# Transposed blocks with joined halves, a new opening and earlier combination in a two-stack transformer kernel

## The chip, the cores and the metric

The kernel runs on one core of a Trainium2 chip. The metric is the device time of one execution in microseconds (us); the figure compared is the median of several runs. A profile is one such execution recorded by the hardware profiler.

## The reference, cut to what matters

256 positions of width 1024 in fp32 go through two stacks of two layers each. In the first stack a layer is FFN, mixer, FFN:

```python
for l in range(DEPTH):                       # DEPTH = 2
    h = h + 0.5 * swiglu(rmsnorm(h, ffn1_norm[l]), ffn1_w_gate[l], ffn1_w_up[l], ffn1_w_down[l])
    u = rmsnorm(h, mix_norm[l])
    z = u @ w_in[l]                          # latent queries/keys, diff q/k/v, pool input, gates
    ...                                      # MLA, differential attention, pooling: three branches
    h = h + merged @ w_out[l]                # gated sum of the branches
    h = h + 0.5 * swiglu(rmsnorm(h, ffn2_norm[l]), ffn2_w_gate[l], ffn2_w_up[l], ffn2_w_down[l])
h = rmsnorm(h, final_norm)

def swiglu(x, w_gate, w_up, w_down):         # D_FF = 2816
    return (jax.nn.silu(x @ w_gate) * (x @ w_up)) @ w_down
```

In the second stack a layer has a mixer of three other branches (gated linear attention, a gated MLP over positions, plain causal attention), and an FFN of width 4096 with the square of relu, `square(relu(h @ w_ff1)) @ w_ff2`, with layer norms between. The weights are some 360 MB, each read once.

## The kernel before, in words

**Precision and products.** The inputs are fp32 and TensorE multiplies in its fp32r format. Every operand is therefore split into a high part (rounded to fp32r) and a low part (the rest), and each product is made of three: low weight x high x, high weight x high x, high weight x low x. For the weights ScalarE writes the high part `wh` (L1694) and VectorE the low part `wl` (L1898, `raw - wh`), in place of the raw data. A unit of weights is 128 x 2048 elements, 1 MB. There are six raw buffers (`NL`) and five high ones (`NH`), so a unit is fetched when the unit six before it is done, and its high part made when the one five before it is done.

**Two forms of product.** The token form (L1455, "tokens") keeps x as the stationary operand, 128 positions by 128 features, and moves 512 weight columns; its result has positions on the partitions. It is used where the result must be so, in the down projections, gates, branches and the first block of each FFN after a norm, and its result is turned by transposes where the next product needs features on the partitions. The transposed form (L1472, "features", planned by `turned_group`) keeps 128 x 128 of the weights stationary and moves x with all its 256 positions; its result has features on the partitions, two groups of 128 features by 256 positions in a PSUM bank. It makes the FFN's hidden values, and the queries and keys of the diff and linear attention (`dqT`, `dkT`, `gqT`, `gkT`) and the linear attention's gate (`ggT`). Its result needs no transposes: ScalarE applies SiLU from PSUM (L1698) or relu (L1702), VectorE multiplies (L1903, L1907) into `mn`, ScalarE and VectorE split that into `mh`, `ml` (L1707, L1913). The down projection reads these. `dqT` and the others are copied by ScalarE (L1749).

**The order.** A planner, `Plan`, writes one list of work items. Each engine's program walks that list and takes its own items, in this order and strictly one after another; waits are on semaphores. `tick()` is called after each block of TensorE work: it runs work put off (`flush`: an item put on `self.later` is run at the second flush after it), lets each of four lanes take a step (`pump`: attention heads, transposes of norms, tables), and puts the next conversions of weights in the list (`advance`: fetches, low parts of those whose high part is in the list, then high parts). In a group of token products `visits` alternates between the two tiles of 128 positions; at the start of a stage four visits of tile 0 come first, at the end of a stage tile 0 is finished first so that its norm runs while TensorE is on tile 1.

**Opening** (`start`). SyncE loads x tile 0, the identity, two units of the gate's weights (these are half units, 512 KB), x tile 1, and so on. GpSimd's queue loads the norm's gain, broadcast to all partitions (L1385). TensorE does twelve transposes of the identity (L1487, "wake"). ScalarE squares (L1720), GpSimd makes the inverse root (L1375, L1379), VectorE scales by it and the gain (L1929), TensorE turns (L1482), ScalarE and VectorE split (L1713, L1917).

**Diff attention** (`diff_pair`). Scores of two heads with two maps each (L1517, L1520) go to four side banks (4 to 7), VectorE takes the maxima (L2034 to L2042), ScalarE the exponentials (L1773, L1775), VectorE combines the two maps (L2047 to L2053, "combine"), TensorE turns the result (L1527) and weighs the values. `latent_kv` makes the keys and values of the MLA branch; its key copies are on VectorE (L2022) and ScalarE (L1768, L1769), and it ends with a tick.

## Time and profile before

| what | value |
| --- | --- |
| median of 3 runs | 2102.19 us (2100.53 to 2102.81) |
| profiled execution, its own time | 2103.13 us |
| span of its first to last instruction | 2101.3 us |
| TensorE busy | 2075.6 us, 99% of the span |
| VectorE, ScalarE, GpSimd busy | 1268.6, 1032.4, 90.5 us |
| mean granted TensorE clock | 0.998 of 2.4 GHz |
| DMA | 375.41 MB, 179 GB/s over the span |

A busy share counts the time in which at least one instruction of the engine was open. Matmuls overlap, so their mean duration is longer than the distance from one to the next. The chain of waits is followed back from the last instruction to what released it, and its pieces on one engine tell how long a number of instructions took in a row.

### The profile page before, as it was taken

How to read it: one execution, taken by the hardware profiler on the slowest of the kernel's cores; microseconds unless marked ns; L12 is line 12 of the kernel's file. 1: busy time of each engine (PE TensorE's matmuls, PEld its weight loads, DVE VectorE, ACT ScalarE, POOL GpSimd, SP SyncE). 2: the span in 40 equal slices, each digit the busy share in tenths (PEclk: the TensorE clock that was granted, in tenths of full speed). 3: DMA queues.
4: the chain of work that ended last, by engine and by line, in shares of the span. 5: the costliest groups of instructions: out<-in, count | busy, mean ns of one | idle time of the engine just before them, and what ended most of it. 6: DMA issues, size and time to landing. Idle time of an engine off the chain costs nothing.

```text
span 2101.3 us, 28959 instructions
## 1 busy us (share of the span) xinstructions
PE 2075.6 (99%) x12424; PEld 1836.6 (87%) x12424; DVE 1268.6 (60%) x1429; ACT 1032.4 (49%) x1301; POOL 90.5 (4%) x123
## 2 busy tenths in 40 slices
PE   7999999999999999999999999999999999999998
PEld 6999978889989898888899989888899888888897
DVE  5555587765455455686654465557755666567555
ACT  5444576454444444675443355643544466445442
POOL 1000100000000001000000000010100000100000
PEclk9999999999999999999999999999999999999999
DMA  8555544465555555444555464544665545455552
GB/s 290 187 182 174 174 146 155 140 211 188 191 193 204 185 185 189 138 150 152 187 202 192 161 226 140 178 142 167 231 193 187 200 143 180 156 172 194 190 190 80
DMA packets 178191, 375.41 MB, mean 179 GB/s; under 512 B 8480, under 2 KB 18848, under 8 KB 178064
## 3 DMA queue, kind: packets, MB, share of 16 engines
q1 hardware_dynamic: 174256, 360.67, 51.7%
q0 software_dynamic: 3808, 12.90, 1.9%
q8 instruction: 98, 1.61, 0.3%
q14 instruction: 29, 0.24, 0.0%
HBM read 372.49 MB, written 1.05 MB: 178 GB/s over the span
## 4 chain that ended last, share of the span: by engine, by line
PE 94%; DVE 2%; DMA 1%; ACT 1%; issue 1%; SPq 0%; POOLq 0%; POOL 0%; DVEq 0%; ACTq 0%
PE pb L1455 56%; PE pb L1472 32%; PE pb L1482 2%; DMA raw<-in_ffn_w_up_dram 1%; PE pb L1527 1%; ACT wh L1694 0%; PE pb L1598 0%; DVE wl L1898 0%; DVE lS L2034 0%; DVE st L2040 0%; DVE st L2039 0%; PE pb L1661 0%; PE pb L1597 0%; PE pb L1620 0%; PE pb L1585 0%
## 5 line engine op out<-in xcount | busy, mean ns | idle before, releaser
L1898 DVE TENSOR_TENSOR wl<-raw,wh 128x2048 fp32r<-128x2048 f32 (+3 forms) x348 | 780.5, 2249 | 286.0 <-ACT wh L1694 285.5
L1694 ACT ACTIVATE wh<-raw 128x2048 fp32r<-128x2048 f32 (+3 forms) x348 | 655.3, 1883 | 501.4 <-PE pb L1455 267.0
L1472 PE MATMUL pb<-xh,wl 128*128 128x256 f32 x1856 | 529.2, 285 | 0.0
L1472 PE MATMUL pb<-xh,wh 128*128 128x256 f32 x1856 | 525.7, 283 | 0.0
L1472 PE MATMUL pb<-xl,wh 128*128 128x256 f32 x1856 | 525.7, 283 | 0.0
L1455 PE MATMUL pb<-wl,xh 128*128 128x512 f32 x928 | 371.7, 400 | 2.5 <-DVE xl L1917 2.5
L1455 PE MATMUL pb<-wh,xl 128*128 128x512 f32 x928 | 362.4, 390 | 0.0
L1455 PE MATMUL pb<-wh,xh 128*128 128x512 f32 x928 | 361.6, 390 | 0.0
L1472 PEld LDWEIGHTS pb<-xh,wl 128*128 128x128 f32 x1856 | 356.8, 192 | 1.4 <-issue 0.7
L1472 PEld LDWEIGHTS pb<-xh,wh 128*128 128x128 f32 x1856 | 356.7, 192 | 0.8
L1472 PEld LDWEIGHTS pb<-xl,wh 128*128 128x128 f32 x1856 | 356.6, 192 | 0.0
L1455 PE MATMUL pb<-wl,mh 128*128 128x512 f32 x736 | 254.6, 392 | 0.2
L1455 PE MATMUL pb<-wh,ml 128*128 128x512 f32 x736 | 252.9, 389 | 0.0
L1455 PE MATMUL pb<-wh,mh 128*128 128x512 f32 x736 | 252.7, 389 | 0.0
L1455 PEld LDWEIGHTS pb<-wl,xh 128*128 128x128 f32 x928 | 175.2, 189 | 40.1 <-issue 3.3
L1455 PEld LDWEIGHTS pb<-wh,xl 128*128 128x128 f32 x928 | 175.0, 189 | 36.7
L1455 PEld LDWEIGHTS pb<-wh,xh 128*128 128x128 f32 x928 | 175.5, 189 | 32.8
L1455 PEld LDWEIGHTS pb<-wh,ml 128*128 128x128 f32 x736 | 138.1, 188 | 29.0
L1455 PEld LDWEIGHTS pb<-wh,mh 128*128 128x128 f32 x736 | 138.2, 188 | 28.4
L1455 PEld LDWEIGHTS pb<-wl,mh 128*128 128x128 f32 x736 | 137.1, 188 | 28.1 <-issue 1.0
L1922 DVE SCALAR_TENSOR_TENSOR h<-pb,h 128x512 f32<-128x512 f32 x72 | 48.1, 686 | 94.9 <-PE pb L1455 94.9
L1707 ACT ACTIVATE mh<-mn 128x512 fp32r<-128x512 f32 x60 | 38.0, 633 | 98.8 <-DVE mn L1903 77.9
(345 smaller groups left out, 1660.5 us busy)
## 6 DMA issues: line engine op xcount, KB each, us to landing
raw<-in_w_in_dram SPq DMA_DIRECT2D x100, 1024.0 KB, 5.2
raw<-in_w_ff_dram SPq DMA_DIRECT2D x64, 1024.0 KB, 5.3
raw<-in_ffn_w_up_dram SPq DMA_DIRECT2D x44, 1024.0 KB, 5.2
raw<-in_ffn_w_down_dram SPq DMA_DIRECT2D x44, 1024.0 KB, 4.9
raw<-in_ffn_w_gate_dram SPq DMA_DIRECT2D x42, 1024.0 KB, 5.2
raw<-in_w_branch_dram SPq DMA_DIRECT2D x24, 1024.0 KB, 5.0
raw<-in_w_out_dram SPq DMA_DIRECT2D x16, 1024.0 KB, 5.0
raw<-in_w_in_dram SPq DMA_DIRECT2D x4, 832.0 KB, 4.4
```

What stands on the lines that cost most here:

```text
L1455: ins = e.matmul(pb[b][:, 0:c1 - c0], x[:, s, cols], w[:, n, c0:c1], start=(it["first"] and n == 0 and q == 0), stop=(it["stop"] and n == ...
L1472: ins = e.matmul(o, w[:, n, c], x[:, it["kk"] + n, :], skip_group_check=True, start=(it["first"] and n == 0 and q == 0 and f % 2 == 0), st ...
L1482: ins = e.transpose(bank[:, c * P:c * P + P], m.tile(it["src"], c), ident[:, :])
L1527: ins = e.transpose(bank[:, c * P:c * P + P], Sb[:, c * P:c * P + P], ident[:, :])
L1694: e.activation(hi, raw, ACT.Copy).then_inc(m.high_done, 1)
L1707: e.activation(m.mh[:, s:s + 2, :].rearrange("p a s -> p (a s)"), m.pair_of(it["src"]), ACT.Copy).then_inc(m.split_high, 1)
L1898: e.tensor_tensor(lo, raw, hi.bitcast(F32), ALU.subtract).then_inc(m.low_done, 1)
L1922: e.scalar_tensor_tensor(o, bank[:, :], it["coef"], o, ALU.mult, ALU.add).then_inc(m.evac[use[0]], 1)
```

## The change

**Joined blocks.** `xh` and `xl` become two halves of one tile `x2` (128 x 8 x 2 x 256). A block ("wide", planned by `wide_group`) is one unit of 8 slots x 256 columns. For each half i of 128 columns there are eight products of the high weight with `xh` and `xl` side by side, 512 columns into a whole bank, and eight of the low weight with `xh`, 256 columns into the bank's first half. VectorE sums the bank's two halves into SBUF ("wadd"). SiLU then runs in place in SBUF ("wsilu"), put off by `later`; "wmul" multiplies; "wrelu" makes relu times itself in one instruction on VectorE; the split into `mh` and `ml` is put off too. `dqT`, `dkT`, `gqT`, `gkT`, `ggT` are written by wadd. The tanh of `ggT` goes through a scratch tile.

**Opening.** TensorE starts with products over 512 columns of a tile of ones ("wake", 4, then 3, then 4). The gain comes as one row of 4 KB through ScalarE's queue and is spread to all partitions by two fp32 products over 512 columns ("spread"); VectorE reads it from PSUM. The identity comes through ScalarE's queue. While `held` is set no conversions are planned by `advance`; `opening` places them and the turns of tile 1. Loads of gains and of the mixer's constants wait for its end and eight pumps (`once_open`).

**Others.** `combine` stands directly behind the softmax items. `latent_kv` ends with a flush and an advance, without a pump. In the last down group of an FFN the column halves alternate inside each group of four slots. A turn of `mn` comes one pump later. Bank choice in the FFNs alternates between main and side banks by quarters of 256 columns.

The diff, cut to its core:

```diff
@@ Memory
-        self.xh = A("xh", take(8192), [P, 8, S], F32R)
-        self.xl = A("xl", take(8192), [P, 8, S], F32R)
+        self.x2 = A("x2", take(16384), [P, 8, 2, S], F32R)
+        self.xh, self.xl = self.x2[:, :, 0, :], self.x2[:, :, 1, :]
...
@@ Plan
+        if self.held:
+            return
         while self.nlo < self.nhi:
             self.add("low", j=self.nlo)
...
-    def turned_group(self, X, keys, banks, epi, base=0, by_bank=True):
...
+    def wide_group(self, key, banks, epi):
+        j = self.take(key)
+        self.split(j)
+        need = self.need("X", range(8), [0, 1])
+        for i in range(2):
+            if i:
                 self.tick()
+            use = self.use(banks[i])
+            v = self.pe("wide", j=j, i=i, use=use, need=need)
+            epi(i, v["p"], use)
+        self.freed[j] = self.x_free = v["p"]
         self.tick()
...
+    def once_open(self, go):
+        def gen():
+            while self.held:
+                yield
+            for _ in range(8):
+                yield
+            go()
+        if self.held:
+            self.lanes[3].append(gen())
+        else:
+            go()
...
-                            for b in range(2) for i in range(size // 2)], end=True)
+                            for i in range(size // 2) for b in range(2)], end=True)
...
+                    for c in range(0, n, 256):
+                        side = (sum(chunks) + n0 - c0 - c) // 256 % 2 == 1
+                        q = c // 256
+                        self.wide_group((gate, (l,), 0, 8, c0 + c, 256), self.pair(0, side), self.gate_w(q))
+                        self.wide_group((up, (l,), 0, 8, c0 + c, 256), self.pair(1, side), self.up_w(q, slot + 2 * q))
...
+    def gate_w(self, q):
+        def epi(i, p, use):
+            self.add("wadd", dst=("sg", q), i=i, p=p, use=use, free=self.sg_free[q])
+            if i:
+                self.silu_n = self.next("silu")
+                self.later.append(lambda: self.add("wsilu", q=q, use=use))
         return epi
+    def up_w(self, q, slot):
+        def epi(i, p, use):
+            self.turn_due(q)
+            self.add("wadd", dst=("mn", q), i=i, p=p, use=use, free=self.mn_free[q])
+            if i:
+                n = self.next("product")
+                self.add("wmul", q=q, use=use, s=self.silu_n)
+                self.split_later(q, slot, n)
+        return epi
...
@@ start
+        self.held = True
+        self.advance()
+        self.pe("wake", n=4)
+        v = self.pe("spread")
+        self.pe("wake", n=3)
+        self.spread = v["p"]
...
+        ready = self.rms(0, g, halves=(0,))
         self.split_next()
+        self.turn("X", 0, 0, ("xn", 0, 0), 4, [ready[0]])
+        self.pe("wake", n=4)
+        self.rms_rest(0, g)
         self.split_next()
         for b in range(2):
             self.square(1, b)
+        self.lanes[0].append(self.opening(g, ready))
+    def opening(self, g, ready):
+        self.turn("X", 4, 0, ("xn", 0, 1), 4, [ready[1]])
+        self.split_next()
+        yield
+        ready = self.rms(1, g, halves=(0,))
+        self.split_next()
+        self.rms_rest(1, g)
+        yield
+        self.turn("X", 0, 1, ("xn", 1, 0), 4, [ready[0]])
+        yield
+        self.turn("X", 4, 1, ("xn", 1, 1), 4, [ready[1]])
+        self.held = False
+        for _ in range(4):
+            yield
         self.add("consts")
...
@@ diff_pair, latent_kv
-        self.quiet = True
-        yield
         for i in range(2):
             c.append(self.next("combined"))
             self.add("combine", i=i, l=l, n=n[2 * i + 1], c=c[i])
+        self.quiet = True
+        yield
...
-        self.tick()
+        self.flush()
+        self.advance()
...
@@ TensorE
+        elif k == "wide":
+            bank, c = pb[use[0]], slice(i * P, i * P + P)
...
+            for s in range(8):
+                e.matmul(bank[:, :], hi[:, s, c], m.x2[:, s, :, :].rearrange("p a s -> p (a s)"), start=(s == 0),
+                         stop=False, skip_group_check=True)
+            for s in range(8):
+                ins = e.matmul(bank[:, 0:S], lo[:, s, c], m.xh[:, s, :], start=False, stop=(s == 7),
+                               skip_group_check=True)
...
+        elif k == "spread":
+            pe.wait_ge(m.first_set, 1)
+            pe.wait_ge(m.row_landed, 16)
+            for q in range(2):
+                ins = e.matmul(pb[1 + 2 * q][:, :], m.first[:, :], m.gain_rows[:, 512 * q:512 * q + 512], start=True, stop=True)
...
@@ ScalarE
+            e.dma_start(m.ident[:, :], m.A["c_ident"]).then_inc(m.ident_landed, 16)
+            a.wait_ge(m.rows_set, 1)
+            e.dma_start(m.gain_rows[0:1, :], m.A["ffn1_norm"][0:1, :]).then_inc(m.row_landed, 16)
...
+            e.activation(m.sg[q][:, :], m.sg[q][:, :], ACT.Silu).then_inc(m.silu_done, 1)
...
@@ VectorE
+        elif k == "wadd":
+            v.pe(p)
+            v.ready(it["free"])
+            e.tensor_reduce(m.half(it["dst"], i), bank[:, :].rearrange("p (a s) -> p s a", a=2), AXX,
+                            ALU.add).then_inc(m.evac[use[0]], 1)
+        elif k == "wmul":
+            q = it["q"]
+            v.emptied(use)
+            v.wait_ge(m.silu_done, it["s"] + 1)
+            e.tensor_tensor(m.mn[q][:, :], m.mn[q][:, :], m.sg[q][:, :], ALU.mult).then_inc(m.product, 1)
+        elif k == "wrelu":
...
+            e.scalar_tensor_tensor(m.mn[q][:, :], m.sg[q][:, :], 0.0, m.sg[q][:, :], ALU.max,
+                                   ALU.mult).then_inc(m.product, 1)
```

## Rows read from the trace of the kernel before

**Rows 1.** The page: span, and busy time of TensorE and its loads.
```profile
span 2101.3 us, 28959 instructions
...
PE 2075.6 (99%) x12424; PEld 1836.6 (87%) x12424; DVE 1268.6 (60%) x1429; ACT 1032.4 (49%) x1301; POOL 90.5 (4%) x123
```

**Rows 2.** The page's groups: line, operation, count, busy us, mean ns, idle before.
```profile
L1472 PE MATMUL pb<-xh,wl 128*128 128x256 f32 x1856 | 529.2, 285 | 0.0
...
L1455 PE MATMUL pb<-wl,xh 128*128 128x512 f32 x928 | 371.7, 400 | 2.5 <-DVE xl L1917 2.5
```

**Rows 3.** Chain of waits, 0 to 320 us: start us, us, what, how many.
```profile
49.50 40.32 PE pb L1472 x336
89.82 32.67 PE pb L1455 x144
122.49 57.59 PE pb L1472 x480
```

**Rows 4.** Waits of TensorE: us in total, times, longest.
```profile
PE pb L1517 <- ACT kT L1769: 4.0, 2, 2.0
PE pb L1455 <- DVE xl L1917: 2.5, 2, 1.4
PE pb L1482 <- DVE xn L1929: 2.4, 1, 2.4
PE pb L1527 <- DVE lS L2053: 2.4, 5, 0.6
PE pb L1482 <- DVE mn L1903: 1.9, 1, 1.9
```

**Rows 5.** VectorE's groups by shape, columns as in the page's groups.
```profile
L1898 DVE TENSOR_TENSOR wl<-raw,wh 128x2048 fp32r<-128x2048 f32 x334 | 761.7, 2287 | 281.6 <-ACT wh L1694 281.2
...
L1903 DVE TENSOR_TENSOR mn<-pb,sg 128x512 f32<-128x512 f32 x44 | 30.4, 690 | 90.2 <-PE pb L1472 86.8 <-PE pb L1455 3.4
...
L2040 DVE TENSOR_REDUCE st<-lS 128x1 f32<-128x256 f32 x56 | 22.9, 409 | 0.0
...
L2039 DVE TENSOR_REDUCE st<-lS 128x1 f32<-128x128 f32 x56 | 16.0, 286 | 1.9
```

**Rows 6.** DMA of a 256-column unit (139.5 to 145), a 512-column one (117 to 122).
```profile
q1 hardware_dynamic: 1040, 1.05, 61.4%
...
raw<-in_ffn_w_gate_dram SPq DMA_DIRECT2D x1, 1024.0 KB, 5.3
...
raw<-in_ffn_w_gate_dram SPq DMA_DIRECT2D x1, 1024.0 KB, 5.2
```

**Rows 7.** Timeline of the opening: start us, us, engine, instruction, idle before and releaser.
```profile
8.80 1.41 DVE L1929 SCALAR_TENSOR_TENSOR xn<-h,st,gain 128x512 f32<-128x512 f32 x2 [8.80 <-DMA gain<-in_ffn_norm_dram]
...
12.69 0.76 PE L1455 MATMUL pb<-wl,xh 128*128 128x512 f32 x1 [1.11 <-DVE xl L1917]
...
22.59 0.50 PE L1455 MATMUL pb<-wl,xh 128*128 128x512 f32 x1 [1.38 <-DVE xl L1917]
...
44.01 1.12 PE L1482 MATMUL pb<-ident,mn 128*128 128x128 f32 x4 [1.92 <-DVE mn L1903]
```

**Rows 8.** Two windows of the opening: busy us of PE, PEld, DVE, ACT, POOL; clock, DMA.
```profile
9.60:22.60 13.00, 10.51 (x41) 8.21 (x41) 10.90 (x12) 11.08 (x15) 7.86 (x18) 1.00 1.00 356
...
41.90:49.50 7.60, 5.68 (x36) 5.50 (x35) 7.41 (x6) 4.22 (x3) 0.00 (x0) 0.78 0.39 145
```

**Rows 9.** Chain of waits, 240 to 256 us: fp32 products over 256 columns.
```profile
246.85 0.86 PE pb L1508 x4
```

**Rows 10.** Timeline of the first diff pair and of the pair after `latent_kv`.
```profile
266.11 2.28 DVE L1898 TENSOR_TENSOR wl<-raw,wh 128x2048 fp32r<-128x2048 f32 x1
...
269.58 0.55 PE L1527 MATMUL pb<-ident,lS 128*128 128x128 f32 x3 [0.34 <-DVE lS L2053]
...
270.71 0.55 PE L1527 MATMUL pb<-ident,lS 128*128 128x128 f32 x3 [0.58 <-DVE lS L2053]
...
283.21 0.50 PE L1517 MATMUL pb<-dkT,dqT 32*128 32x128 f32 x8 [1.98 <-ACT kT L1769]
```

**Rows 11.** DMA issues of the run: how many, KB each, median us to landing.
```profile
ident<-in_c_ident_dram SPq DMA_DIRECT2D x1, 64.0 KB, 3.2
```

More of the change, by code:

```diff
@@ L555, in hadd, with rms @@
             self.h_ready[t] = [self.h_half[t, 0], self.h_half[t, 1]]
-    def rms(self, t, gain, final=False):
+    def rms(self, t, gain, final=False, halves=(0, 1)):
         n = self.next("normed", 2)
-        self.add("rms", t=t, gain=gain, final=final, sq=self.count["squared"], n=n, c=self.next("rstd"))
+        self.add("rms", t=t, gain=gain, final=final, sq=self.count["squared"], n=n, c=self.next("rstd"), halves=halves,
+                 spread=self.spread if gain == 0 else None)
         self.gain_user[gain % 2] = n + 2
@@ L563, in rms, with rms_rest @@
         return [("normed", n + 1), ("normed", n + 2)]
+    def rms_rest(self, t, gain):
+        self.add("rms", t=t, gain=gain, final=False, c=self.count["rstd"] - 1, halves=(1,),
+                 spread=self.spread)
     def square(self, t, b):
@@ L691, in relu2, with relu_w @@
         self.sg_free[i] = ("evac", use)
-    def relu_f(self, slot):
+    def relu_w(self, q, slot):
         def epi(i, p, use):
-            self.relu2(i, p, use)
-            self.mn_free[i] = self.split_into(slot + 2 * i, ("mn", i), ("evac", use))
+            self.add("wadd", dst=("sg", q), i=i, p=p, use=use, free=self.sg_free[q])
+            if i:
+                self.turn_due(q)
+                n = self.next("product")
+                self.add("wrelu", q=q, use=use, free=self.mn_free[q])
+                self.split_later(q, slot, n)
         return epi
@@ L1001, in mixer1 @@
         qk = []
[L1002 to L1005 removed]
+        self.copy_w(416, "dqT", qk)
+        self.copy_w(928, "dkT", qk)
         self.dqk = list(qk)
@@ L1185, in mixer2, with silu_g @@
         self.lanes[3].append(decay())
[L1186 removed]
+        self.group(self.cols(W, l, 1024, 1, self.copy_t("gv", gv)))
         self.gq, self.gk, self.gv = gq, gk, gv
[L1189 to L1193 removed]
+        for q in range(2):
+            def silu_g(i, p, use, q=q):
+                self.add("wadd", dst=("ggT", q), i=i, p=p, use=use, free=None)
+                if i:
+                    n = self.next("gate_half")
+                    self.later.append(lambda: self.add("gsilu", q=q, use=use, n=n))
+                    gg.append(("gg_ready", n + 1))
+                    self.g_free[0] = ("gg_ready", n + 1)
+            self.wide_group((W, (l,), 0, 8, 1536 + 256 * q, 256), self.pair(q), silu_g)
         while not self.decayed:
@@ L1894, in dve_program @@
         bank = pb[use[0]] if use else None
-        if k == "low":
+        if k == "load" and t == 0:
+            e.memset(m.fill[:, :].bitcast(F32), 1.0).then_inc(m.fill_set, 1)
+            v.step(e.memset(m.first[:, :], 0.0))
+            v.own_steps()
+            e.memset(m.first[0:1, :], 1.0).then_inc(m.first_set, 1)
+        elif k == "low":
             raw, hi, lo = m.halves(it["j"])
```

189 lines of the change are left out of this document (82 added, 107 removed).

## The prediction

> **What bounds the kernel now.** I read the page first. TensorE is busy for 2075.6 of 2101.3 us [rows 1], so the question is not who waits but how long its own stream of instructions is. Busy time does not answer that, since matmuls overlap: the reader sees 285 ns for a matmul over 256 columns and 400 ns for one over 512 [rows 2]. The chain of waits gives the true pace, because in the long stretches it runs along TensorE alone. There 336 matmuls over 256 columns take 40.32 us and 480 take 57.59 us, which is 120.0 ns each; 144 over 512 columns take 32.67 us, 226.9 ns each [rows 3]. At the granted 2.4 GHz the columns alone would be 106.7 and 213.3 ns. So each matmul costs its columns plus about 13.3 to 13.6 ns, whatever its width. The waits of TensorE are next [rows 4]: after the first 22 us they add up to some 9 us, in three places (the transposes of a diff pair, the map scores behind kT, the first turn of mn). So what shortens the kernel is fewer TensorE instructions, and these few waits; VectorE and ScalarE matter only where they would become late.
>
> **The products.** The three-product form (lo·xh, hi·xh, hi·xl) of a transposed block has 1856 triples of 256 columns (three groups of 1856 [rows 2]). Because xh and xl now lie side by side per slot, hi·xh and hi·xl become one product over 512 columns. A triple costs 3 x 120.0 = 360.0 ns now, and 226.9 + 120.0 = 346.9 ns afterwards [rows 3]. The difference of 13.1 ns times 1856 is 24.3 us. Nothing hides it, as TensorE idles nowhere in these stretches. The bounds: the least is 0, if the joined product ran at the pace of two products over 256 columns (240 ns); the most is 1856 x 13.6 = 25.2 us. I take 24.3, since the row of a product over 512 columns with the same 128x128 stationary shape is there, and it differs only in which operand moves.
>
> The Trainium skill (TensorE: Matmul & The Clock Gate, section "Wait — 56ns, not 53.3ns?") puts the fixed cost of a warm matmul at about 2.5 ns. By that rule removing 1856 instructions would be worth an estimated 4.6 us, not 24.3. The rows of this case show about 13 ns at both widths, and I go by them.
>
> **What VectorE gets.** Each of the 116 blocks (1856 / 16 matmuls of each kind) is now emptied in two halves by a sum over the pair, 232 tensor_reduce from PSUM, 512 elements in and 256 out. The trace has no such form. From below: the reductions of 128 and 256 elements take 286 and 409 ns [rows 5], a slope of 0.96 ns per element, so 512 is 655 ns. From above: 409 ns doubled with all of its fixed part is 0.82 us, and if the two-element inner loop were to cost twice per element, 655 + 246 x 2 is about 1.15 us. I take 0.7 us, by the nearest row in size, since the multiplication of 512 elements from PSUM takes 690 ns [rows 5]. The multiplication (wmul) or square (wrelu) stays at 0.69, now beside the sum rather than in its place. Per gate/up quarter, that is two blocks of 16 x 346.9 ns = 5.55 us each, VectorE then does 2 x 2.29 (the low halves of the weights [rows 5]) + 4 x 0.7 + 0.69 + 0.69 (ml) = 8.8 us against 11.1 us. In the relu blocks two quarters are 4.58 + 2.8 + 2 x 0.69 + 2 x 0.69 = 10.1 against 11.1 us. Thus VectorE becomes 80 to 91% full there but not the bound: cost 0. The cover is that low halves are made up to five blocks ahead, and that the banks alternate: gate [0,2], up [1,3], and 4 to 7 for the odd quarter, so a bank is asked for again some 22 us later in the gate/up blocks and 11 us in the others. If the sum cost over 0.95 us, this cover would be used up in the relu blocks first.
>
> The deferral (SiLU a block later, msplit two ticks and mlow four ticks after the product) costs nothing at the end of a stage either: the last quarter's slots are asked for after at least four token visits of 12 x 226.9 ns = 2.7 us, 10.9 us in all, while its work (0.7 + 0.7 + the high copy ahead of it in ScalarE's queue, 1.9 + 0.6 + 0.7) takes some 5 us. Swapping the order of halves and columns in the last down group is what gives the FFN that room; it moves only the first half's hadd and square to one visit before the end, still ahead of the second half's.
>
> **The weights' transfers.** A block is now 8 slots x 256 columns, rows of 1 KB, in place of 4 x 512, rows of 2 KB. Such units exist already (the third chunk of 256): 1040 packets land in 5.3 us, against 5.2 us with 528 [rows 6]. The load of a unit is issued a block and more before ScalarE asks for it. Cost 0; bounds 0 to 1 us, as SP waits on TensorE in any case.
>
> **The opening.** Now: the gain, broadcast by GpSimd's queue, lands at 8.80 us and only then VectorE scales; the first real product starts at 12.69; at 22.59 TensorE has waited for xl of the second tile; at 44.01 it has idled 1.92 us for mn [rows 7], and runs at a mean 0.78 of the clock from 41.9 to 49.5 [rows 8]. Afterwards the gain row is 4 KB on ScalarE's queue behind the identity and behind GpSimd's memset. With the 3.2 us of the identity's landing [rows 11] it is there at some 5.3 us, and two fp32 products over 512 columns spread it. Four fp32 products over 256 take 0.86 us at the full clock [rows 9], so these two take 0.9 us, or 1.7 at half clock: scaling can start near 7 instead of 8.80. It doesn't all count: the raw unit 0 lands at about 9 (0.5 MB less before it), and its high and low copy come before, so the first product is at 11.8, 0.9 us early. Second, conversions of units 4 and on are held until the second tile is turned; the 2.3 us low half that stood before that xl goes behind it: 1.4 us of wait gone. Third, the mixer's constants and gains (their broadcasts kept the queues full from 9.6 to 22.6: DMA share 1.00 [rows 8]) go out after the opening, so the weights of the first transposed block land earlier, and the turn of mn comes a tick later: 1.9 us of idle gone, and with it the half clock behind it, 1.2 us (eleven products at 213 instead of 120 ns, and the transposes). The sum is 0.9 + 1.4 + 1.9 + 1.2 = 5.4 us. Bounds: 0, if VectorE's chain (4 scalings, 4 low halves, 4 splits, about 10.5 us in series) sets the end anyway; 8 us, if the filling products also take away the half clock before 16.7 us. Added on the queues moved past: ScalarE issues two DMAs and waits for the memset before its first square, which waits for x until 4.2 us anyway.
>
> **The mixers.** latent_kv no longer pumps the lanes: the map scores are issued one visit later, and the gate's token product goes ahead, whose bank 0 has been emptied by VectorE's first kT copy. TensorE's two waits of 1.98 us [rows 4, 10] go: 4.0 us; bounds 0 and 4.0. The combination stands right behind the maxima and ahead of the next low half (2.28 us at 266.11 [rows 10]), so the transposes at 269.58 and 270.71 find it done. It waits for the exponentials, which end 0.9 us after the last maximum, and behind it a low half is held for 2.2 us, with blocks in hand. Of 2.4 us of waits [rows 4] I take 1.6; bounds 2.4 saved and 2 lost. dqT, dkT and ggT lose their ScalarE copies and get sums on VectorE, under products of 5.55 us per block: 0.
>
> **Sum.** 24.3 + 5.4 + 4.0 + 1.6 = 35.3 us. The profiled execution took 2103.1 us (span 2101.3 and 1.8 around it), 0.9 above the median of the runs; 2103.1 - 35.3 = 2067.8, and against the median 2102.2 - 35.3 = 2066.9. I forecast 2067.
>
> **Rivals.**
> 1. The products gain, the waits only move (mn's stall returns as another wait of the opening, the scores wait for bank 0). For it: each of these waits is short, and VectorE's chain lies close behind. Against: the named releasers are really taken away. Time: 2102.2 - 24.3 = 2078.
> 2. The 13 ns do not go with the instruction: the joined product takes 240 ns. Against it: the 226.9 ns of the token products. For: there x is the stationary operand, here it moves. Time: 2102.2 - 11.0 = 2091. With the page's 2.5 ns it would be an estimated 2087.
> 3. Slower: VectorE becomes the bound of the transposed blocks. It decides from 0.95 us per sum in the relu blocks and 1.28 us in the gate/up quarters ((11.1 - 5.96) / 4). At 1.8 us a quarter takes 13.2 us on VectorE, 2.1 over; 36 quarters are 75 us, and the down groups in between, where VectorE idles more than half, give back some half; the relu quarters add (2 x 2.29 + 7.2 + 2.76 = 14.5 against 11.1) 3.4 x 12 = 41, half given back. Together 58 lost against 35 won: 2125. For it: a form that no row shows. Against: the slope of 0.96 ns.
>
> **How the numbers follow.** Forecast 0.70, rival 1 0.20, rival 2 0.04, rival 3 0.04, better than the forecast's own bounds 0.02. Range 2058 to 2082: down to the sum of the upper bounds (25.2 + 8 + 4 + 2.4 = 39.6, thus 2063) and a little for waits that I do not see, up past rival 1. The bound of a measurable change is 0.2%, 4.2 us. Faster 0.94, same 0.02, slower 0.04.
>
> **What would show it.** The pace of joined products in the chain: 227 ns, and 16 + 16 of both kinds in 5.55 us. The reduction's mean: about 0.7 us. No TensorE wait for kT, nor over 0.3 us for a combination. First product near 11.8 and none of the stall before 44. VectorE's share near 68 to 70%. I'd be wrong with a reduction above 1 us, a joined product above 230 ns, or TensorE waits that name the sum, wmul or the high copy.

## The result

The kernel after takes 2072.03 us (median of 4 runs, 2071.5 to 2072.52) beside 2102.34 us of before (2100.53 to 2102.81): a ratio of 0.9857, 95% interval 0.984 to 0.9874. The forecast was 2067 us in a range of 2058 to 2082. Of 35.3 us forecast, 30.3 us came by the medians and 30.6 us by the profiled spans, 2101.3 and 2070.7 us. The same kernel was measured again with the experiments:

> The changed kernel itself, as the yardstick for the kernels beside it on the same chip: 2072 us, 30 us less than the kernel before. In its profile the joined products again take 1.84 us for eight and each half block 2.793 us.

It took 2071.82 us (2071.76 to 2072.51), ratio 0.9856 (0.9842 to 0.9869), span 2070.7. Spans below are set against this 2070.7, medians against this 2071.82.

### The profile page after: what moved, and what is told of

Read it like the earlier page. It is cut to its first block, busy times and chain, and to the rows that moved or that the text cites. A ratio compares the mean times of both kernels' runs of the same rounds, so it can differ in the third digit from the quotient of the medians.

```text
span 2070.7 us, 25612 instructions
## 1 busy us (share of the span) xinstructions
PE 2054.7 (99%) x10571; PEld 1736.3 (84%) x10571; DVE 1407.6 (68%) x1664; ACT 1013.6 (49%) x1261; POOL 90.6 (4%) x123
## 3 DMA queue, kind: packets, MB, share of 16 engines
q8 instruction: 84, 1.38, 0.3%
HBM read 371.97 MB, written 1.05 MB: 180 GB/s over the span
## 4 chain that ended last, share of the span: by engine, by line
PE 98%; DVE 1%; ACT 0%; DMA 0%; issue 0%; POOL 0%; POOLq 0%; DVEq 0%
PE pb L1529 58%; PE pb L1540 21%; PE pb L1543 11%; PE pb L1552 2%; PE pb L1603 1%; PE pb L1674 1%; PE pb L1673 0%; DVE wl L1986 0%; PE pb L1611 0%; PE pb L1612 0%; PE pb L1737 0%; PE pb L1610 0%; PE pb L1661 0%; ACT wh L1774 0%; DMA gain_rows<-in_ffn_norm_dram 0%; PE pb L1696 0%
## 5 line engine op out<-in xcount | busy, mean ns | idle before, releaser
L1529 PE MATMUL pb<-wh,x 128*128 128x512 f32 x1856 | 571.0, 389 | 0.0
L1540 PE MATMUL pb<-x,wh 128*128 128x512 f32 x1856 | 468.2, 394 | 0.0
L1529 PEld LDWEIGHTS pb<-wh,x 128*128 128x128 f32 x1856 | 348.8, 188 | 68.7
L1540 PEld LDWEIGHTS pb<-x,wh 128*128 128x128 f32 x1856 | 335.0, 189 | 61.6 <-issue 0.7
L1529 PE MATMUL pb<-wl,x 128*128 128x512 f32 x928 | 370.4, 399 | 2.0 <-DVE wl L1986 1.5
L1543 PEld LDWEIGHTS pb<-x,wl 128*128 128x128 f32 x1856 | 253.2, 190 | 18.3
L1543 PE MATMUL pb<-x,wl 128*128 128x256 f32 x1856 | 258.7, 282 | 0.0
L1529 PEld LDWEIGHTS pb<-wl,x 128*128 128x128 f32 x928 | 174.4, 188 | 40.1 <-issue 4.3
L2000 DVE TENSOR_REDUCE sg<-pb 128x256 f32<-128x512 f32 x120 | 82.3, 686 | 44.0 <-PE pb L1543 43.9
L1529 PE MATMUL pb<-wl,yph 128*128 128x512 f32 x128 | 51.3, 401 | 0.0
```

Source lines behind the costliest of these rows:

```text
L1529: ins = e.matmul(pb[b][:, 0:c1 - c0], x[:, s, cols], w[:, n, c0:c1], start=(it["first"] and n == 0 and q == 0), stop=(it["stop"] and n == ...
L1540: e.matmul(bank[:, :], hi[:, s, c], m.x2[:, s, :, :].rearrange("p a s -> p (a s)"), start=(s == 0), stop=False, skip_group_check=True)
L1543: ins = e.matmul(bank[:, 0:S], lo[:, s, c], m.xh[:, s, :], start=False, stop=(s == 7), skip_group_check=True)
L2000: e.tensor_reduce(m.half(it["dst"], i), bank[:, :].rearrange("p (a s) -> p s a", a=2), AXX, ALU.add).then_inc(m.evac[use[0]], 1)
```

## The profile after

The page, span, busy times and the groups that answer to [rows 1, 2, 5]:

```profile
span 2070.7 us, 25612 instructions
...
PE 2054.7 (99%) x10571; PEld 1736.3 (84%) x10571; DVE 1407.6 (68%) x1664; ACT 1013.6 (49%) x1261; POOL 90.6 (4%) x123
...
L1540 PE MATMUL pb<-x,wh 128*128 128x512 f32 x1856 | 468.2, 394 | 0.0
L1543 PE MATMUL pb<-x,wl 128*128 128x256 f32 x1856 | 258.7, 282 | 0.0
...
L2000 DVE TENSOR_REDUCE sg<-pb 128x256 f32<-128x512 f32 x120 | 82.3, 686 | 44.0 <-PE pb L1543 43.9
```

TensorE still fills the span. The sum of the pair on VectorE, the form that no row of before had, takes 686 ns, and VectorE waits for TensorE's banks ahead of it, not the other way round. The waits of TensorE in the kernel after (columns as in [rows 4]):

```profile
PE pb L1563 <- DMA gain_rows<-in_ffn_norm_dram: 2.6, 1, 2.6
PE pb L1673 <- ACT lQ L1885: 2.3, 2, 1.2
PE pb L1529 <- DVE wl L1986: 1.5, 1, 1.5
PE pb L1557 <- DVE fill L1979: 1.4, 1, 1.4
PE pb L1529 <- DVE x L2021: 0.5, 1, 0.5
```

Those for kT, for the combination lS and for mn [rows 4] are gone; of the 2.5 us for xl, which is now a half of x2 and goes by the name x, 0.5 us are left. Two waits are new: one for lQ in the mixers (2.3 us in two), and one for wl in the opening (1.5 us), which is taken up below. The chain of waits shows the pace of the blocks: eight joined products, then eight narrow ones, then the next half.

```profile
48.24 1.85 PE pb L1540 x8
50.09 0.95 PE pb L1543 x8
...
84.57 32.67 PE pb L1529 x144
```

A half block takes some 1.84 + 0.95 = 2.79 us, while the token products keep their 226.9 ns (32.67 / 144), as in [rows 3]. Had the joined product run at that pace, eight of each kind would take 8 x 346.9 = 2775 ns. The start times of single products show where the rest is. Median ns from one start to the next in the half blocks that follow another half block, computed from the trace of the kernel after:

```
512 columns (after narrow ones): 233 236 228 232 231 227 227 227
256 columns (after joined ones): 113 119 120 120 120 120 120 120
sum 2793; before: 24 x 120.0 = 2880
```

The first five joined products behind narrow ones are 25 to 28 ns longer in all, and the first two narrow ones some 8 ns shorter. The half blocks directly behind token products, which are 512 wide too, take 2766 ns, without the extra. Those behind transposes, which are 128 wide, show it (231, 231, 236, 228, 233 ns from the second product on).

The gain over the kernel before, from the start of the n-th token product in both traces, before minus after: −0.9 us at the first, 0.3 at product 48, 5.3 at 96 (behind the first transposed blocks), 7.4 at 480, 10.4 at 1148 (behind the first layer's mixer; inside a mixer the two orders of work differ, and the n-th products can't be compared), 30.6 at the end. In three parts this is: the wide blocks 232 x 87 ns = 20.2 us; the opening 3.9 us; the mixers 6.4 us (2.7 in the first layer, 3.7 in the second). The sum is 30.5.

The opening, by the chain of waits of the kernel after:

```profile
1.71 4.32 DMA gain_rows<-in_ffn_norm_dram
...
6.16 3.75 PE pb L1563 x4
9.91 1.28 PE pb L1557 x3
...
13.55 0.47 PE pb L1529
```

and by its timeline (TensorE's rows and one of VectorE's; columns as in [rows 7]):

```profile
10.99 1.05 PE L1552 MATMUL pb<-ident,xn 128*128 128x128 f32 x4
...
10.03 0.75 DVE L2036 SCALAR_TENSOR_TENSOR xn<-h,st,pb 128x512 f32<-128x512 f32 x1 [8.25 <-PE pb L1563]
...
18.52 0.50 PE L1529 MATMUL pb<-wl,x 128*128 128x512 f32 x1 [1.50 <-DVE wl L1986]
...
38.85 1.98 PE L1540 MATMUL pb<-x,wh 128*128 128x512 f32 x8
...
44.41 0.60 PE L1552 MATMUL pb<-ident,mn 128*128 128x128 f32 x4
```

The first real product starts at 13.55, which is 0.86 us later than before, not 0.9 earlier; yet the first wide block starts at 38.85, against 39.05 before. The turn of mn at 44.41 has no idle time ahead of it.

The row at 18.52 is the new wait. The thirteenth product needs a low half of weights that VectorE makes from 17.24 us; its high half ScalarE makes from 16.15 us, behind the split of x at 15.66, which waited for the turn that TensorE started at 15.02. The first 24 products, with the waits and turns among them, take 8.65 us (13.55 to 22.20), against 9.90 before (12.69 to 22.59). They start some 230 ns apart from the first on, where the first nine before were 427 ns apart, which wins 1.8 us; the wait of 1.38 us for xl is gone, the one of 1.50 for wl is new, and four more transposes stand among them (0.4 us). The windows that answer to [rows 8] (columns as there):

```profile
9.60:22.60 13.00, 10.95 (x50) 8.32 (x49) 9.42 (x11) 7.18 (x12) 5.29 (x13) 1.00 0.79 268
41.90:49.50 7.60, 7.60 (x47) 6.70 (x46) 7.53 (x8) 5.52 (x5) 0.00 (x0) 1.00 0.69 224
```

The second window shows TensorE busy throughout and the granted clock at 1.00, where before it idled for 1.9 us and had a mean of 0.78. The first shows the queues no longer full (a DMA share of 0.79 in place of 1.00).

The mixers lost time before that no wait names. In the second layer's mixer of the kernel before, soon after the wait of 1.98 us for kT that ended at 882.20 us, stands this window (columns as in [rows 8]):

```profile
883.70:887.12 3.42, 3.42 (x10) 2.65 (x9) 3.21 (x13) 1.97 (x8) 0.00 (x0) 0.50 0.28 108
```

TensorE worked through it at half the clock, and its products of 512 columns started 425 to 430 ns apart in place of 227: some 1.7 us lost. The first layer's wait for kT was as long and has no such stretch behind it, and the kernel after has none in either mixer (a clock of 1.00 from 222 to 443 and from 811 to 1032 us). This accounts for most of the mixers' 6.4 us: of the waits 6.8 us are gone (4.0 for kT, 2.4 for the combination, 0.4 for an lS of ScalarE) and 2.3 for lQ are new, which is 4.5, and 1.7 of half clock makes 6.2. It also explains why the second layer's mixer won more than the first's.

## Experiments

All are variants of the kernel after. A span is that of one profiled execution, and its opening varies where the code does not: in the eight kernels with the opening unchanged (the repeat, and those of this section outside "The opening") the first product starts between 12.47 and 13.40 us, and at 13.55 in the kernel after. The landing of the gain row makes up to 0.5 us of this (the spread starts between 5.69 and 6.16). The rest is TensorE's pace: the first turn's four transposes take 1.05 us in the kernel after (10.99, above), which are 0.21 us apart, and 0.66 us in the kernel with the product taken apart, 0.11 us apart, since its pace rose earlier:

```profile
10.52 0.66 PE L1553 MATMUL pb<-ident,xn 128*128 128x128 f32 x4
```

So the profiled kernel after has the latest opening of them all, and each span is read with the time of its first product and beside the medians of the runs. Neither is exact: the repeat's first product is 0.2 us earlier than that of the kernel after, and its span the same; and the kernel before, measured again with each batch of experiments, had medians of 2101.34 to 2102.08 us, so medians of different batches are comparable to some 0.7 us.

### The pace of the joined product

**The joined product taken apart again.** The sums on VectorE, the layout and the order stay; only the instruction is two.

```diff
-e.matmul(bank[:, :], hi[:, s, c], m.x2[:, s, :, :]..., start=(s == 0), ...)
+for a in range(2):
+    e.matmul(bank[:, a * S:a * S + S], hi[:, s, c], m.x2[:, s, a, :], start=(s == 0 and a == 0), ...)
```

> The changed kernel with the joined product taken apart again: high weight x high part and high weight x low part as two products over 256 columns each, everything else as changed. My theory (each matmul costs about 13 ns beside its columns, and the join removes 1856 of them, less a loss of about 18 ns per half block at the step from narrow to wide products) expects a half block of 24 x 120.0 = 2.880 us and a total 232 x 87 ns = 20.2 us above the changed kernel, about 2092. The rival, that the gain comes from the opening, the mixers and the different staging and not from the join, expects less than 5 us above it.

2090.99 us (2090.8 to 2091.25), ratio 0.9946 (0.9933 to 0.996), span 2089.2: 18.5 us lost, and the opening is 0.9 us earlier, so 19.4 us in the blocks (19.2 by the medians). Its chain:

```profile
50.52 1.92 PE pb L1541 x16
52.44 0.96 PE pb L1544 x8
```

Every product is back at 120 ns, and the half block at 2.88 us. So the saving is that of 1856 products, 10.5 ns each and not 13.1. Every product has its own load of the stationary operand (PEld counts as many as PE, 10571, and 12427 with the product taken apart), so the runs do not tell the cost of a product from that of its load.

**Narrow products first, then the joined ones.** Is the extra the joined product's own (then it stays at the start of the half) or that of the step from narrow to wide?

```diff
-for s in range(8): hi . x2 (512 columns)
-for s in range(8): lo . xh (256 columns)
+for s in range(8): lo . xh (256 columns)
+for s in range(8): hi . x2 (512 columns)
```

> The order inside a half block turned round: eight products over 256 columns first (low weight), then eight over 512 (high weight x both parts). Theory A, that the 28 ns extra over the first five wide products belong to the step from 256 to 512 columns, expects the gaps 233, 236, 229, 232, 231 behind the ninth product of each block, and a total within 1 us of the changed kernel. Rival B, that they belong to the start of a block (its wait, its new bank), expects the wide products at 227 throughout and the extra time, if any, on the narrow ones.

2071.57 us (2071.2 to 2072.02), ratio 0.9854 (0.9841 to 0.9868), span 2070.2. The chain, where L1540 is now the narrow product:

```profile
120.79 1.84 PE pb L1543 x8
122.63 0.95 PE pb L1540 x8
```

The gaps 233, 236, 228, 232, 231 ns now belong to the ninth to thirteenth product, and the half block is 2793 ns as in the kernel after. The extra follows the step, not the place in the half nor the opening of a bank.

**Mirrored halves.** Half 0 joined then narrow, half 1 narrow then joined: one step up and one down per block in place of two each.

```diff
+for n, part in enumerate((high, low) if i == 0 else (low, high)):
+    ins = part(n == 0)
```

> The first half of a block runs its wide products and then the narrow ones, the second half the narrow ones and then the wide ones, so that equal widths meet in runs of 16 and the step from narrow to wide comes once per block instead of twice (116 fewer). Theory A expects 116 x 28 ns = 3.2 us less than the changed kernel. Rival B (cost of a block's start) expects no difference beyond 0.5 us.

2069.43 us (2068.97 to 2069.76), ratio 0.9844 (0.983 to 0.9857), span 2067.5: 3.2 us won, of which 1.0 is an earlier opening (2.4 us by the medians).

```profile
51.87 1.91 PE pb L1547 x16
53.78 3.65 PE pb L1541 x16
```

L1547 is the narrow product, L1541 the joined one: sixteen of a kind now stand together. The halves take 2766 and 2801 ns, 5567 in place of 5586 for a block: 19 ns x 116 = 2.2 us, less than the 28 ns x 116 = 3.2 us that the extras alone would give, since the 8 ns of the step down go with them.

### The mixers

**The lanes pumped in latent_kv again.**

```diff
-        self.flush()
-        self.advance()
+        self.tick()
```

> The changed kernel with the tick at the end of latent_kv put back (so the lanes are pumped there and the next map scores are issued directly behind the key products). If the gain of the first mixers (2.7 us in layer 0, 3.7 us in layer 1 by comparing the traces) comes from letting the gate's product go ahead of them, TensorE waits 1.98 us for kT twice again and the total is 3 to 4.5 us above the changed kernel. The rival, that the waits only moved (1.2 us twice for lQ in the changed kernel), expects under 2 us.

2078.07 us (2075.91 to 2078.84), ratio 0.9884 (0.9869 to 0.9899), span 2075.6: 4.9 us lost with an opening 0.6 earlier, so 5.5 in the mixers (6.25 by the medians), more than the 3 to 4.5 expected. The trace names the place, and has a window at half clock in the second layer's mixer (columns as in [rows 4], then as in [rows 8]):

```profile
PE pb L1592 <- ACT kT L1849: 4.9, 2, 2.5
...
864.29:871.12 6.83, 6.54 (x28) 4.85 (x29) 5.35 (x18) 2.89 (x12) 0.00 (x0) 0.50 0.35 136
```

The wait of 2.46 us that ends at 864.58 lies ahead of it. By the start times of the token products the first layer's mixer loses 1.3 us and the second's 4.3, with a wait for kT of the same length in both, so about half of this profiled execution's loss is the slower pace.

**The combination put back behind a yield.**

```diff
+        self.quiet = True
+        yield
         for i in range(2):
             c.append(self.next("combined"))
             self.add("combine", i=i, l=l, n=n[2 * i + 1], c=c[i])
-        self.quiet = True
-        yield
```

> The changed kernel with the combination of a diff pair a tick later again, behind a low half of the weights. My theory expects TensorE's waits for the combination (0.3 and 0.6 us per pair, 2.4 us in all in the kernel before) to come back: 1.5 to 3 us above the changed kernel. The rival, that other waits take it up, expects under 1 us.

2079.51 us (2078.57 to 2080.57), ratio 0.9893 (0.9878 to 0.9908), span 2076.8: 6.1 us lost with an opening 0.7 earlier, so 6.8 in the mixers (7.7 by the medians), over twice the most that was expected. Its clock is 1.00 in both mixers. TensorE's waits name the combination:

```profile
PE pb L1603 <- DVE lS L2160: 7.4, 12, 1.3
```

The timeline of this kernel at the first diff pair:

```profile
257.87 2.28 DVE L1986 TENSOR_TENSOR wl<-raw,wh 128x2048 fp32r<-128x2048 f32 x1
...
262.47 0.55 PE L1603 MATMUL pb<-ident,lS 128*128 128x128 f32 x3 [0.58 <-DVE lS L2160]
```

The same pair in the kernel after:

```profile
260.61 0.48 DVE L2160 SCALAR_TENSOR_TENSOR lS<-lS,st,lS 128x256 f32<-128x256 f32 x1
261.01 2.28 DVE L1986 TENSOR_TENSOR wl<-raw,wh 128x2048 fp32r<-128x2048 f32 x1
...
261.70 0.81 PE L1603 MATMUL pb<-ident,lS 128*128 128x128 f32 x6
```

The low half of 2.28 us goes ahead of the combination in the one and behind it in the other; the six transposes find their operand ready. But the wait for the combination was 2.4 us in the kernel before [rows 4] and is 7.4 us here, so the wait of the kernel before doesn't tell what this edit is worth.

**Both undone.**

```diff
(both edits above)
```

> Both mixer edits undone, the pump at the end of latent_kv and the combination a tick later; blocks and opening as changed. Undone alone, the pump cost 4.9 us of the span and the combination 6.1. The comparison of the traces gave the two together 6.4 us over both first mixers. If they share one benefit (with the pump back, the combination's place moves too), this kernel is about 6.4 us above the changed one, with the waits of the kernel before: 4.0 us for kT and 2.4 us for the combination. If they add up, it is 11 us above.

2078.36 us (2078.06 to 2078.68), ratio 0.9888 (0.9871 to 0.9904), span 2076.3. The opening was 1.1 us earlier, so the mixers lose 6.7 us (6.5 by the medians); its granted clock is 0.50 from 275.46 to 278.88 us, in the first layer's mixer this time. Two of its waits of TensorE:

```profile
PE pb L1592 <- ACT kT L1849: 4.0, 2, 2.0
...
PE pb L1602 <- DVE lS L2159: 2.4, 5, 0.6
```

These are the waits of before [rows 4] to the tenth of a microsecond. With the openings taken out, the edits undone alone cost 5.5 and 6.8 us, and together 6.7: they don't add, and with the combination back, putting the pump back costs nothing more. Half clock does not explain it: without its two stretches (an estimated 3.0 us in the first, by which its second layer lost more than its first, and 1.7 in this one, half of its 3.4) the three would be about 2.5, 6.8 and 5.0. Why they don't add is open; I did not follow which instruction meets which for every pair, so only the sum of the two edits stands.

### VectorE's new work

**The sum issued twice.** Each sum is repeated from the same bank.

```diff
+            v.step(e.tensor_reduce(m.half(it["dst"], i), bank[:, :].rearrange("p (a s) -> p s a", a=2), AXX, ALU.add))
+            v.own_steps()
```

> Every sum of a bank's halves is done twice on VectorE (the same result), 1.4 to 1.45 us in place of 0.69 before a bank is given back. This is the condition of the slower rival: it was said to decide from 0.95 us in the relu blocks and from 1.28 in the gate/up quarters. By that sum VectorE needs 12.9 against 11.2 us per relu chunk and 11.5 against 11.2 per gate/up quarter: up to 12 x 1.7 + 36 x 0.3 = 31 us above the changed kernel if nothing is in hand. My theory, that low halves made up to five blocks ahead and the down groups behind take up most of it, expects 0 to 10 us. If VectorE had no cover at all, each half block would be longer by 0.7 us, 160 us in all.

2077.28 us (2077.09 to 2077.63), ratio 0.9882 (0.9868 to 0.9897), span 2075.6: 4.9 us lost, with an opening 0.5 earlier (5.5 by the medians). The page's line of busy times:

```profile
PE 2056.3 (99%) x10571; PEld 1736.2 (84%) x10571; DVE 1559.9 (75%) x1896; ACT 1017.5 (49%) x1261; POOL 90.8 (4%) x123
```

Two of its waits of TensorE that the kernel after does not have:

```profile
PE pb L1529 <- DVE sg L2003: 2.3, 4, 0.7
...
PE pb L1688 <- DVE zv L2219: 1.0, 2, 0.5
```

VectorE has 152 us more to do, and 147 of them stay hidden; the half blocks stay at 2793 ns. So at 1.37 us per sum (2 x 0.686) the bound is not reached. Part of what shows are waits behind a block's last sums (sg 2.3, zv 1.0, ml 0.5 us), up to 0.7 us each time. The third rival put the point of decision at 0.95 us in the relu blocks; that point is refuted, as the doubled sum lies above it and the blocks kept their pace. Twelve half blocks of relu in a row, in the kernel after and with the sum doubled (columns as in [rows 8]):

```profile
1561.90:1595.60 33.70, 33.70 (x194) 29.67 (x194) 27.68 (x29) 14.44 (x11) 0.00 (x0) 1.00 0.57 188
1564.70:1598.40 33.70, 33.70 (x195) 29.66 (x194) 32.35 (x38) 14.68 (x11) 0.00 (x0) 1.00 0.55 188
```

VectorE is busy for 32.35 of 33.70 us, 96%, and was for 27.68. The forecast's sum for such blocks with 1.37 us per sum, 4.58 + 4 x 1.37 + 2.76 = 12.8 us against 11.1, would be 115%. So part of this work falls outside the stretch. That blocks in hand and VectorE's idle time in the groups around take it up is argued; how far it reaches was not measured.

### The opening

**The filling products left out.**

```diff
-        self.pe("wake", n=4)
...
-        self.pe("wake", n=3)
...
-        self.pe("wake", n=4)
```

> The changed kernel without the eleven filling products of the opening; the spread of the gain stays. If the fills are what puts the first real products at the full clock (they start at 13.55 us with 227 to 236 ns between them, where the kernel before had 427 ns until 16.6 us), they run at 427 ns again for some 3 us. Whether that costs anything is the question: if VectorE's chain of low halves and splits sets the pace until 22 us, the total is within 1 us of the changed kernel; if TensorE does, it is 2 to 3 us above.

2072.87 us (2072.65 to 2073.45), ratio 0.9862 (0.9845 to 0.9878), span 2071.1. Its first product in the timeline:

```profile
12.64 0.75 PE L1526 MATMUL pb<-wl,x 128*128 128x512 f32 x1 [1.50 <-DVE x L2018]
```

and the window from it on (columns as in [rows 8]):

```profile
12.60:15.90 3.30, 3.26 (x9) 2.60 (x10) 1.69 (x2) 1.34 (x5) 1.78 (x4) 0.51 1.05 384
```

The kernel after in its own first 3.3 us of products:

```profile
13.50:16.80 3.30, 3.25 (x16) 2.57 (x16) 2.20 (x3) 2.49 (x7) 1.76 (x4) 1.00 0.80 292
```

Without the fills the first product is 0.9 us earlier, but the granted clock is a mean 0.51 until 15.9 us, that is 1.2 GHz, and 9 instructions (transposes among them) are recorded where the filled kernel has 16; by the first wide block it is 0.7 us behind. The fills trade a later start for the full clock, and win 0.4 to 0.7 us by the traces, 1.05 by the medians. Ahead of its first change the clock's column can't be read: it says 1.00 in a window of this kernel from 5.90 to 9.70 us too, where the products of the spread ran at half the pace of [rows 9], and in the kernel before from 12.60 to 16.70, where 10 products took 4.1 us. There the pace is the evidence: the first products of the kernel after start 230 ns apart.

**The spread in two halves.** Each scaling waits for its own product only.

```diff
-        v = self.pe("spread")
-        self.spread = v["p"]
+        self.spread = [self.pe("spread", q=q)["p"] for q in range(2)]
...
+                    v.pe(it["spread"][b])
```

> The spread of the gain is two items, and the scaling of each half of x waits only for its own one. In the changed kernel the two fp32 products over 512 columns took 6.16 to 9.91 us (four passes of 0.9 us at half clock), where I had counted 1.7 us, and the first scaling started at 10.03 in place of 7. The first scaling should start about 1.9 us earlier, near 8.2, and the first product near 11.7 in place of 13.55. If VectorE's chain sets the end of the opening, 1 to 2 us less in total than the changed kernel; if the late transfers of the weights set it, 0.

2071.26 us (2070.94 to 2072.11), ratio 0.9851 (0.9835 to 0.9868), span 2070.3, 0.4 won (0.6 by the medians) where 1 to 2 were expected. Its timeline, TensorE's rows and then VectorE's:

```profile
8.66 2.27 PE L1556 MATMUL pb<-fill 128*128 128x512 f32 x3
10.73 0.69 PE L1551 MATMUL pb<-ident,xn 128*128 128x128 f32 x4
12.93 0.47 PE L1528 MATMUL pb<-wl,x 128*128 128x512 f32 x1 [0.57 <-DVE x L2020]
...
8.05 0.75 DVE L2036 SCALAR_TENSOR_TENSOR xn<-h,st,pb 128x512 f32<-128x512 f32 x1 [6.28 <-PE pb L1562]
```

The first scaling is 2 us earlier, yet the turn that needs it stands behind three fills in TensorE's own queue and starts at 10.73. The first product at 12.93 lies inside the 12.47 to 13.55 of the kernels whose opening is unchanged, so no gain of this edit by itself is shown.

**The row alone.** In addition the product contracts over one partition, so no memset of the other 127 rows is needed, and the row's DMA goes ahead of the identity's.

```diff
-            e.matmul(pb[1 + 2 * q], m.first[:, :], m.gain_rows[:, 512 * q:512 * q + 512], ...)
+            e.matmul(pb[1 + 2 * q], m.first[0:1, :], m.gain_rows[0:1, 512 * q:512 * q + 512], ...)
...
-            e.memset(m.gain_rows[:, :], 0.0).then_inc(m.rows_set, 1)
...
-            e.dma_start(m.ident[:, :], m.A["c_ident"]).then_inc(m.ident_landed, 16)
-            a.wait_ge(m.rows_set, 1)
             e.dma_start(m.gain_rows[0:1, :], m.A["ffn1_norm"][0:1, :]).then_inc(m.row_landed, 16)
+            e.dma_start(m.ident[:, :], m.A["c_ident"]).then_inc(m.ident_landed, 16)
```

> As the spread in halves, and the products contract over the one partition that holds the row, so no tile has to be zeroed first: the row's DMA is issued at 0.7 us in place of 1.7 us, ahead of the identity's. The row should land about 1 us earlier (near 5.1) and everything behind it as well: first scaling near 7.2, unless the inverse root is later; 0.5 to 1 us less than the spread in halves if it is still the row that is waited for, 0 otherwise.

2070.34 us (2070.03 to 2070.72), ratio 0.9848 (0.9833 to 0.9862), span 2068.2, 2.5 won against the span of the kernel after and 1.5 by the medians; against the spread in halves 2.1 and 0.9. Its timeline, TensorE's rows and then VectorE's:

```profile
3.45 3.78 PE L1561 MATMUL pb<-gain_rows,first 1*128 1x512 f32 x4
7.16 1.65 PE L1555 MATMUL pb<-fill 128*128 128x512 f32 x3
...
11.17 0.47 PE L1527 MATMUL pb<-wl,x 128*128 128x512 f32 x1 [0.30 <-DVE x L2016]
...
6.77 0.75 DVE L2032 SCALAR_TENSOR_TENSOR xn<-h,st,pb 128x512 f32<-128x512 f32 x1 [5.25 <-POOL st L1452]
```

The spread starts at 3.45, right behind the first four fills, in place of 6.16: the row had landed by then, 1.6 us before the 5.1 expected. It takes as long (3.78 us) with one partition as with 128. The first product at 11.17 is 1.3 to 2.4 us earlier than in the kernels with the unchanged opening, and what is gained there is kept to the end. VectorE's first scaling now waits for GpSimd's st and ends at 7.52, but that is not the next term: the turn that needs it stands behind the three fills and starts at 8.61.

**The row and the mirror together.**

> The spread in halves from one partition together with the mirrored order of wide and narrow products. If both gains are real and independent, the sum of the two: about 2067 us, 35 us below the kernel before.

2067.87 us (2067.56 to 2068.16), ratio 0.9836 (0.9821 to 0.985), span 2066.1. By the medians the two gains add (1.5 and 2.4 us alone, 3.95 together), and this is the fastest version of the study.

## Why the prediction was right or wrong

**The bound: right.** TensorE's stream of instructions sets the time. Of 30.6 us, two thirds are the removed products. The forecast's sum was 4.8 us too high: products 4.1 and opening 1.5 too much, mixers 0.8 too little.

**The products: mechanism right, term too large.** "I take 24.3" was 13.1 ns x 1856; measured were 20.2 us, and 19.4 by taking the product apart. I argued that the joined product differs from the token product only in the operand that moves, and took a pace from a stretch where all products are 512 wide. Here widths alternate eight by eight, and each step up costs 25 to 28 ns, less 8 at the step down; the mirrored halves show the cost as that of the step. The joined products' mean is 230.1 ns, just at the 230 named as a sign of being wrong. Extra and giveback leave about 18 ns per half block, and 18 ns x 232 = 4.2 us is the missing 4.1. What inside TensorE makes the step cost is open: the runs show where it falls, not why. The rule of the Trainium skill (TensorE: Matmul & The Clock Gate, section "Wait — 56ns, not 53.3ns?") of about 2.5 ns of fixed cost per warm matmul would have made this an estimated 4.6 us; the 19.4 us of the first experiment decide against it for these products, each with its own load.

**VectorE: right.** 0.7 us taken, 686 ns measured; share 68% against 68 to 70; no wait of TensorE names the sum, wmul or the high copy. The stated margin was too small: twice the sum still left the blocks' pace alone.

**The transfers: right.** The transfers land as the rows of before had it (36 of these 42 are of 8 slots x 256 columns):

```profile
raw<-in_ffn_w_gate_dram SPq DMA_DIRECT2D x42, 1024.0 KB, 5.3
```

**The opening: the step with the most wrong in it.** 5.4 us forecast, 3.9 measured, and by other terms. "The first product is at 11.8, 0.9 us early" failed: it starts at 13.55, 0.86 late. Three parts of that step failed: the row landed at 6.03, not 5.3; the spread took 3.75 us, not 0.9 to 1.7; and the filling products were ahead of the turn in TensorE's queue, which I had not counted. Its premise failed as well: raw unit 0 was to land at about 9 us and set the pace, but ScalarE starts on it at 6.08, against 9.62 before, so the first product hung on the spread, the turn and VectorE's order alone. The second is a misreading of a row: `x4` in [rows 9] is not four products. An fp32 product is recorded as two matmuls, so 0.86 us is two products over 256 columns; the two products over 512 columns of the spread are 0.86 x 2 = 1.7 us at 2.4 GHz, and 3.4 at 1.2 GHz. The same row, read rightly, would have come near the 3.75. The one-row run shows that shortening this chain is paid in full: 2.4 us at the first product, 2.5 at the end, against the same trace. The second part, the wait for the second tile's xl, went, but the wait of 1.50 us for wl came; the full pace of the first products made up for it (1.8 us), which the forecast had only in its upper bound. In all the kernel after makes up 1.2 us between the first product and product 48 (−0.9 to 0.3), which the late start had used. The third came in full: at product 96 it is 5.25 us ahead, of which 0.2 were there at the first wide block and 16 x 0.087 = 1.4 are the half blocks' own; 3.7 remain for mn's idle time and the half clock behind it, against 1.9 + 1.2 = 3.1 forecast. No run takes back the held conversions, the late constants or the later turn one by one, so that these removed the waits is argued from the traces of before and after.

**The mixers: right in kind, 6.4 against 5.6 us.** The waits named in the forecast vanished, and by the edits that it named (undoing the two brings back 4.0 and 2.4 us). My split of 4.0 and 1.6 is not a property of the edits: alone they cost 5.5 and 6.8. A new wait of 2.3 us for lQ appeared, which I had not counted, and 1.7 us of half clock behind a wait for kT went, which I had not counted either; the 6.4 is near the 5.6 partly because these two nearly cancel.

**The rivals.** The first (the waits only move, 2078) did not hold, since the named waits left and only 2.3 us came in their place. The second (a joined product of 240 ns, 2091) is what the kernel with the product taken apart does, at 2090.99; the joined one runs at 227 to 236 ns. The meeting of 2091 and 2090.99 is in part luck, as opening and mixers were forecast at 11.0 and gave 10.3 us. The third did not come even with the sum doubled.

## What to carry to other kernels

A pace taken from a long stretch of one width is right for that stretch only: where widths alternate, read the gaps at the changes, and order the work so that equal widths stand together. Read a count in the profile (`x4`) against the number of instructions in the code before you turn it into a duration per instruction. And what is ahead of an instruction in its own engine's queue (here the filling products) can hide a gain that its operand's producer has made. Compare experiments with each other only after taking out what varies without the edit (here when the opening's pace rises, and stretches at half clock).

## What the runs showed of the hardware

- A step from products over 256 columns to ones over 512 costs 25 to 28 ns, spread over the first five (233, 236, 228, 232, 231 against 227 ns); the step down gives back 8 ns (113, 119 against 120). It follows the step whichever kind stands first.
- Waits of the same length don't always lower the clock: behind 1.98 us without work, the kernel before had 3.4 us at a granted 0.50 in one mixer and none in the other.
- An fp32 product is recorded as two matmuls, and takes as long with one contracted partition (3.78 us for two products over 512 columns) as with 128 (3.75 us).
- Nine instructions in 3.3 us at a granted clock of 0.51 against 16 in the same time in the kernel with filling products, whose first real products start 230 ns apart: the opening's pace depends on what TensorE did just before (fills until some 13.0 us in the one, 1.5 us without work in the other).
- A 1 MB transfer in rows of 1 KB took 5.3 us against 5.2 us in rows of 2 KB.
